# A gated linear recurrence's softplus, begun one product of a convolution earlier

## The reference, cut to what matters

```
xc = conv4(xr) + conv_b                       # depthwise, over 4 tokens
r = sigmoid(xh @ w_a + b_a)                   # xh: xc by heads of 64
i = sigmoid(xh @ w_x + b_x)
log_a = -LRU_C * r * softplus(-lam)           # lam: 1024 parameters
a = exp(log_a)
b_in = sqrt(-expm1(2 * log_a)) * (i * xc)
h = scan(h' = a * h + b_in)
...
blocks = t[:, :, blk_idx] + pe                # compress(t), t = k_cmp, v_cmp
return gelu(blocks.reshape(...) @ w1) @ w2
```

## Time and profile before

| what | value |
|---|---|
| median of 3 runs | 2501.0 us (2500.04 to 2501.87) |
| profiled execution, device time | 2500.24 us |
| profiled execution, span | 2498.4 us |
| TensorE busy | 2482.8 us, 99% of the span |
| VectorE, ScalarE, GpSimd busy | 46%, 42%, 45% |
| mean granted TensorE clock | 0.999 |

### The profile page before, as it was taken

One profiled execution on the slowest core, in us unless ns is written; L12 is line 12 of the kernel. 1 busy time (PEld: TensorE's weight loads), 2 busy tenths in 40 slices (PEclk: granted clock), 3 DMA queues, 4 the chain that ended last, 5 costly groups with the idle time before them and its releaser, 6 DMA issues.

```text
span 2498.4 us, 33197 instructions
## 1 busy us (share of the span) xinstructions
PE 2482.8 (99%) x13326; PEld 2144.2 (86%) x13326; DVE 1138.5 (46%) x2332; ACT 1041.5 (42%) x2014; POOL 1131.3 (45%) x651
## 2 busy tenths in 40 slices
PE   9999999999999999999999999999999999999998
PEld 8888898888889888889888888888898888888887
DVE  7681487755415642325244455523334335445313
ACT  7553487742325332235344333333344333333323
POOL 3354455544445554444443445444543445444442
PEclk9999999999999999999999999999999999999999
DMA  5233322245332553332222222222322222222232
GB/s 213 76 102 106 97 78 73 64 166 197 128 134 77 202 190 113 102 106 75 102 85 80 81 81 93 81 93 93 110 92 85 77 84 89 81 89 81 93 101 76
DMA packets 89240, 258.86 MB, mean 104 GB/s; under 512 B 8960, under 2 KB 30208, under 8 KB 88704
## 3 DMA queue, kind: packets, MB, share of 16 engines
q1 hardware_dynamic: 89088, 256.74, 30.9%
HBM read 246.22 MB, written 2.10 MB: 99 GB/s over the span
## 4 chain that ended last, share of the span: by engine, by line
PE 91%; DVE 4%; ACT 3%; issue 1%; POOL 1%; DMA 0%; DVEq 0%; SPq 0%; POOLq 0%; ACTq 0%
PE bank L1795 88%; PE bank L1805 3%; ACT PP L2013 0%; DVE Y L2315 0%; POOL n L2875 0%; DVE pt_lo L2315 0%; ACT Hhi L2013 0%; DVE C L2315 0%; DVE nt L2315 0%; ACT w_hi L2013 0%; DVE XC L2323 0%; ACT blkv L2013 0%; ACT blkk L2013 0%; DVE PP L2575 0%; ACT pt_hi L2013 0%
## 5 line engine op out<-in xcount | busy, mean ns | idle before, releaser
L2870 POOL TENSOR_TENSOR w_lo<-w_raw,w_hi 128x1024 fp32r<-128x1024 f32 (+1 forms) x302 | 743.7, 2465 | 849.5 <-ACT w_hi L2013 849.2
L1795 PE MATMUL bank<-Hhi,w_hi 128*128 128x512 f32 (+1 forms) x1700 | 657.0, 386 | 0.0
L1795 PE MATMUL bank<-Hlo,w_hi 128*128 128x512 f32 (+1 forms) x1700 | 651.2, 383 | 0.1
L1795 PE MATMUL bank<-Hhi,w_lo 128*128 128x512 f32 (+1 forms) x1700 | 651.2, 383 | 0.0
L2013 ACT ACTIVATE w_hi<-w_raw 128x1024 fp32r<-128x1024 f32 (+1 forms) x318 | 326.0, 1029 | 117.1 <-DMA w_raw<-in_wa 82.7
L1795 PEld LDWEIGHTS bank<-Hhi,w_lo 128*128 128x128 f32 x1700 | 319.6, 188 | 63.5
L1795 PEld LDWEIGHTS bank<-Hlo,w_hi 128*128 128x128 f32 x1700 | 320.1, 188 | 57.6 <-POOL w_lo L2870 0.5
L1795 PEld LDWEIGHTS bank<-Hhi,w_hi 128*128 128x128 f32 x1700 | 320.0, 188 | 56.6
L2870 POOL TENSOR_TENSOR w_fifth_lo<-w_fifth_raw,w_fifth_hi 128x1024 fp32r<-128x1024 f32 x77 | 192.0, 2493 | 231.5 <-ACT w_fifth_hi L2013 231.5
L1795 PE MATMUL bank<-Hhi,w_fifth_hi 128*128 128x512 f32 x404 | 161.3, 399 | 0.0
L1795 PE MATMUL bank<-Hhi,w_fifth_lo 128*128 128x512 f32 x404 | 157.7, 390 | 0.0
(11 more groups left out here) (415 smaller groups left out, 4820.8 us busy)
## 6 DMA issues: line engine op xcount, KB each, us to landing
w_raw<-in_wb SPq DMA_DIRECT2D x169, 512.0 KB, 3.4
w_raw<-in_wa SPq DMA_DIRECT2D x139, 512.0 KB, 3.4
wm<-in_w_ada SPq DMA_DIRECT2D x48, 512.0 KB, 4.5
w_fifth_raw<-in_wb SPq DMA_DIRECT2D x42, 512.0 KB, 3.4
w_fifth_raw<-in_wa SPq DMA_DIRECT2D x35, 512.0 KB, 3.4
QQ<-Y SPq DMA_DIRECT2D x64, 128.0 KB, 2.4
wa_raw<-in_wb SPq DMA_DIRECT2D x5, 512.0 KB, 6.0
XR<-in_x SPq DMA_DIRECT2D x4, 512.0 KB, 6.7
```

The costliest lines, as they stand in the source:

```text
L1795: return self.e.matmul(o, lhs, rhs, start=start, stop=stop)
L2870: self.e.tensor_tensor(x.lo[:, k:k + n, :], x.raw[:, k:k + n, :], f(x.hi[:, k:k + n, :]), ALU.subtract).then_inc(*w_rest(s, k))
```

## The change

The softplus becomes known to the background tasks one product earlier. Each of its instructions stands 8 tiles earlier in the queues of VectorE and ScalarE. `soft_begin` comes with the first tile of product 1, no longer with that of product 2. No instruction is added or removed, and no other queue is touched.

```diff
@@ -1406,7 +1406,7 @@
 
             self.gated = [False] * KT
             for j in range(KT):
-                if j == 2:
+                if j == 1:
                     t_soft = self.later(self.softplus())
                 self.run(self.product(H, ("conv", j), self.evac_conv(j)))
                 if j > 1:
```

## The result

The kernel before took 2501.8 us (2500.04 to 2504.49, 21 runs), the changed kernel 2505.62 us (2503.84 to 2508.08, 21 runs). The ratio is 1.0016, with a 95% interval of 1.0010 to 1.0022: slower by 3.8 us, which is under 0.2%. The forecast was +3.7 us on another base (2501.0), so 2504.7; the range held the time.

The account below looks back on a forecast made before the run. TensorE, busy 99%, was taken as the bound, its longest wait 1.6 us for ScalarE's `TR`. 2.43 + 1.5 - 0.24 = +3.7 us on 2500.24 gave 2503.9, with 0.76 for the median 2504.7 us; range 2500.5 to 2506.3.

Parts of the forecast that it names:

- Step 1: VectorE behind `xs_lo` of product 0: the three first tiny operations run undisturbed by about 48.3, before GpSimd's slab at 49.57.
- Step 2: ScalarE behind `w_fifth_hi`: table load of 1.28 us to 51.74, Exp of 0.21 us, VectorE's addition starting at 52.00.
- Step 3: VectorE's addition behind the Exp: caught by 0.1 us by GpSimd's `w_fifth_lo`, begun at 51.89, and ending at 54.34.
- Step 4: `conv(1)` starts at 54.91, `xs_hi` of product 1 at 58.10, 2.72 us later; product 3 doesn't wait for its bank.
- Step 5: VectorE behind `xs_lo` of product 1: the third tiny operation, at 59.76, meets GpSimd's slab of 59.74 and takes 2.38 us.
- Step 6: `conv(2)` starts at 62.86, `xs_hi` of product 2 at 66.05, +2.43 us; TensorE waits 4.1 us in place of 1.6.
- Step 7: Downstream: VectorE's lateness ends before product 4's `conv`, later steps cost nothing; the `kc` wait grows some 0.2 us or vanishes.
- The clock: TensorE's granted clock falls in the new wait, to near half speed; loss between nothing and 2.95 us, taken as 1.5.
- both meetings, the clock holds: Rival: TensorE waits 2.43 us more, about 0.2 us more at `kc`, without a clock loss: 2503.6 us; chance 0.17.
- One meeting is missed: Rival: VectorE escapes one slab; only the first missed +1.3 us, only the second +0.2 us; chance 0.17.
- None is met: Rival: VectorE's tiny operations meet no slab and the earlier start relieves `conv(2)`, -0.9 us: 2500.1 us; chance 0.10.
- slower by over 0.2%: Rival: TensorE's clock stays low for long, +5.4 us at 5.9 us of slow work: 2506.4 us; chance 0.12.

Follow-up runs that it names:

- start0: Changed kernel with the softplus beginning at product 0's first tile, one product earlier still; 2505.63 us, ratio 1.0014 to the kernel before.
- filler2: Changed kernel with 4 and 10 unused constant-tile matmuls filling TensorE's waits ahead of g(1, 0) and g(1, 1); 2502.96 us, ratio 1.0007 to the kernel before.
- hold_slab: Changed kernel in which no slab is cut with product 2's first tile, but some tiles later; 2502.04 us, ratio 1.0004 to the kernel before.
- short_after: Changed kernel with GpSimd's slabs of products 1 and 2 cut into four instructions each; 2504.89 us, ratio 1.0014 to the kernel before.
- late_add: Changed kernel with the softplus's addition, reciprocal and `soft_z` moved behind `xs_lo` of product 1, the Exp left in place; 2505.23 us, ratio 1.0016 to the kernel before.
- block1: Changed kernel, softplus still beginning with product 1, with all steps from `soft_z` on emitted together; 2506.4 us, ratio 1.0017 to the kernel before.
- start4: Changed kernel with the softplus beginning at product 4's first tile; 2504.76 us, ratio 1.0013 to the kernel before.
- short_before: Kernel before the change with GpSimd's slabs of products 1 and 2 cut into four instructions each; 2502.54 us, ratio 1.0006 to the kernel before.
- filler: Changed kernel with 8 and 20 unused constant-tile matmuls put into TensorE's waits ahead of g(1, 0) and g(1, 1); 2505.71 us, ratio 1.0018 to the kernel before.
- start3: Changed kernel with the softplus beginning at product 3's first tile; 2500.75 us, ratio 0.9995 to the kernel before.
- block4: Changed kernel with the softplus beginning at product 4 and its steps from `soft_z` on emitted together; 2499.07 us, ratio 0.9991 to the kernel before.
- block4b: The same kernel as block4, timed once more; 2499.6 us, ratio 0.9992 to the kernel before.

## Why the prediction was right, point by point

Where a forecast time stands beside a measured one, the 0.6 us of the later start are taken off the measured one. Times in brackets and those of the clock are as the trace counts.

- *Step 1, the first three operations undisturbed:* they ran behind `xs_lo` of product 0 at 0.14 to 0.17 us each. Right.
- *Step 2, the Exp behind table load and `w_fifth_hi`:* forecast 51.74, measured 51.75 (52.35).
- *Step 3, the addition caught by 0.1 us:* it began 0.11 us after the slab and took 2.32 us, forecast 2.34.
- *Step 4:* `conv(1)` forecast at 54.91, measured 54.87; `xs_hi` of product 1 forecast at 58.10, measured 58.06. Product 3 didn't wait for its bank.
- *Step 5, the second meeting with a margin of 0.02 us:* it came with exactly that margin (60.34 against 60.32), 2.40 us. The traces speak against luck in this margin: both engines start from the same `xs_hi`, and the same 0.02 us stands in the trace before and in start0's, 0.01 in filler2's.
- *Step 6:* `xs_hi` of product 2 forecast at 66.05, measured 66.05; g(1, 1) forecast at 69.85, measured 69.84, so +2.41 us for the +2.43 forecast. The two waits were put at 4.1 us and are 3.75 by the profile. The difference is mostly how the modelled ends of matmuls are counted, since the start behind the waits is where it was forecast.
- *Step 7:* the wait for `kc` is gone. That the later tiny operations cost nothing was right too, but they weren't undisturbed: `xs_lo` of product 3 took 2.29 us and the next one 2.31. `kc` ended at 79.2 (as the trace counts), 1.4 us before TensorE wanted it. With TensorE earlier by that much it isn't free, as hold_slab shows.
- *The clock:* taken as the middle of 0 and 2.95, 1.5 us; filler2 measures 1.56. That the size came out so closely is luck: the prediction had no row for how long the clock stays low after such a gap, and its own bounds left 3 us open. What it had wrong is the moment. It let the clock fall in the wait; it held through both waits and fell at about 71.8 us (the stretch of 71 to 72 is at 0.90), 1.4 us after g(1, 1) had resumed. That distance isn't fixed: the fall came 0.7 us after the resumption in short_after, 0.3 to 0.5 us after it in late_add, start0 and block1, and 0.1 us before it in start4. By the Trainium skill, "TensorE: Matmul & The Clock Gate", section "HAM oscillation — how this bites in real kernels", work after a gap starts cold. The trace agrees that gaps cost a stretch of slow work, and differs in that the first 1.4 us of that work still ran at 1.00.
- *The sum:* +3.7 forecast; +3.64 in the stage, +3.8 in the medians. The stage is the sounder match: how often the second fall of the clock comes in the runs of each kernel isn't known, and the medians hold it.

Of the rivals, "both meetings, the clock holds" is what filler2 makes by force: forecast +2.6 in all, its stage is +2.36. "One meeting is missed" is borne out in one half: with the first out of the way (late_add), `xs_hi` of product 1 starts where ScalarE's `blkv` ends, forecast 57.0, measured 56.85 once its own start offset of 0.43 us is taken off. At the next `xs_hi` 1.1 us were forecast to be won; late_add won 0.4 and spent some 0.8 on the operations that it moved there. The other half, only the second missed, is hold_slab: `xs_hi` of product 2 forecast at 63.84, measured 63.77 with its 1.05 us of later start taken off. But the +0.2 us forecast for it became +1.28 in the stage, since the slabs held back made the wait for `kc` that the forecast hadn't. "None is met" was priced at -0.9 us. It wasn't tried with both meetings removed at the change's place. Of the whole, the stretch of slow clock was 3.4 us (by the windows, 71.8 to 75.2), so it stayed below the 5.2 us from which "slower by over 0.2%" would have decided.

## What to carry to other kernels

In this kernel a single operation of 0.2 us can cost 2.4 us, if it stands in VectorE's queue where GpSimd works on a slab and something on TensorE's path stands behind it. So the place to look for isn't the earliest one but a stretch in which VectorE's next important operation is itself waiting for TensorE; put all of them there at once and check where the last one ends, since spread out they reach the next crowded place. And when a wait is removed by shifting someone else's work, follow that work: hold_slab and start4 cut the wait at 67 us to 0.8 us and to nothing and got one of 2.2 to 2.8 us elsewhere.

## What the runs showed of the hardware

- A burst of short GpSimd instructions lets VectorE have one operation for each, 0.65 to 0.72 us apiece (short_after, short_before). By the Trainium skill, "SBUF — State Buffer", section "Who interferes with whom", whoever issues first holds the shared port pair for its whole instruction. The trace agrees. Held were TENSOR_SCALAR, TENSOR_TENSOR and, in start4, a SCALAR_TENSOR_TENSOR of 128 x 8 (2.32 us); of the large ones `xs_lo`, a TENSOR_TENSOR of two SBUF tiles, took 2.29 us in place of 0.69. `conv(3)`'s SCALAR_TENSOR_TENSORs, which add a bank and an SBUF tile, run in the changed kernel at 69.85 to 72.17 beside a slab of 69.89 and take 2.32 us for three, as without one.
- The granted clock fell behind single waits of 2.46 us (start0), 2.53 (block1) and 2.76 (start4), and behind pairs of waits, 1.00 and 2.75 (the change), 0.43 and 2.91 (short_after), 0.60 and 2.75 (late_add). It held through 1.6 (before), 1.9 (short_before) and 2.16 us (hold_slab). In the changed kernel it then stood at 0.50, the 1.2 GHz level, from 71.8 to 75.2 us, and this cost 1.56 us by filler2.
- A second fall comes far behind the change. Behind 12 matmuls of one column at 1162 to 1168 us, where TensorE waits 0.4 us in each trace, the clock went to 0.50 in the changed kernel, filler, short_after, short_before, late_add, start0 and block1, and stayed at 1.00 in the kernel before, filler2, hold_slab, start3, start4 and both block4 runs. Why it falls in some is open, and so is whether it is tied to the first: of the six traces with a fall between 50 and 130 us five have it, of the eight without two. It is worth some 1.5 us. Of 21 runs of the kernel before (those beside block1 and block4b) 12 have a mean clock of 0.999 and a mean time of 2501.05 us, 9 have 0.998 and 2502.53 us. One such fall more or less would make that difference; whether it does, no trace here shows. Two profiled executions can so differ by more than the change between them, as here, 5.7 us against 3.64; the stage had to be measured by itself.
